# Gate and up of the second block's experts loaded whole: one 2 MB transfer each, each into its own slot, both slots freed together

## The reference

```python
def expert(x_e, w_gate, w_up, w_down):      # x_e: the tokens that chose this expert
    g = x_e @ w_gate                        # 1024 x 512, 2 MB
    u = x_e @ w_up                          # 1024 x 512, 2 MB
    return (silu(g) * u) @ w_down           # 512 x 1024, 2 MB
# out[token] += gate_weight * expert(...) for the two experts of each token
```

## Time and profile before

| | us |
|---|---|
| median of 3 runs | 2060.79 (2059.64 to 2061.04) |
| the profiled execution | 2061.98 |
| its span, first to last instruction | 2060.2 |
| TensorE busy | 1902.1 (92%) |
| second block's expert stage, first gate and up product to the last down product | 1557.8 to 2051 |

### The profile page before, as it was taken

One profiled execution on the slowest core, in us unless ns is written; L12 is line 12 of the kernel. 1 busy time (PEld: TensorE's weight loads), 2 busy tenths in 40 slices (PEclk: granted clock), 3 DMA queues, 4 the chain that ended last, 5 costly groups with the idle time before them and its releaser, 6 DMA issues.

```text
span 2060.2 us, 20805 instructions
## 1 busy us (share of the span) xinstructions
PE 1902.1 (92%) x8230; PEld 777.2 (38%) x8230; DVE 442.4 (21%) x1029; ACT 282.2 (14%) x534; POOL 22.4 (1%) x87
## 2 busy tenths in 40 slices
PE   7778999999999999999999888989988999999998
PEld 3443333333333333333333335647543333333333
DVE  1622111111111111111111123236522111111111
ACT  1311111111111111111111011130011111111111
POOL 3000000000000000000000000000000000000000
PEclk9888999999999999999999989999999999999999
DMA  9325999999999999999999473330244999999996
GB/s 304 154 97 213 412 408 415 410 407 416 412 407 413 410 410 408 416 411 408 415 410 407 209 274 134 128 118 1 82 166 174 400 414 404 409 404 419 403 410 249
DMA packets 82971, 667.63 MB, mean 324 GB/s; under 512 B 10384, under 2 KB 12192, under 8 KB 32640
## 3 DMA queue, kind: packets, MB, share of 16 engines
q1 hardware_dynamic: 78176, 664.84, 79.8%
q10 hardware_dynamic: 4416, 1.49, 0.3%
q0 software_dynamic: 352, 0.93, 0.2%
HBM read 666.19 MB, written 1.05 MB: 324 GB/s over the span
## 4 chain that ended last, share of the span: by engine, by line
PE 92%; ACT 4%; DVE 3%; issue 1%; DMA 0%; DVEq 0%; SPq 0%; ACTq 0%
PE ps L1299 54%; PE ps L1446 10%; PE ps L1359 6%; PE ps L1285 6%; PE ps L1180 3%; PE ps L1293 2%; PE ps L1249 1%; PE ps L1337 1%; PE ps L1330 1%; ACT Z L506 1%; ACT scr L510 1%; PE ps L1569 1%; PE ps L1164 1%; PE ps L1580 1%; PE ps L1603 1%
## 5 line engine op out<-in xcount | busy, mean ns | idle before, releaser
L1299 PE MATMUL ps<-ring,Z 128*64 128x512 f32 x4704 | 1051.2, 598 | 20.6 <-ACT Z L502 18.1
L1299 PEld LDWEIGHTS ps<-ring,Z 128*64 128x64 f32 x4704 | 342.3, 138 | 674.3 <-issue 648.2
L1359 PE MATMUL ps<-Z 64*128 64x512 f32 x520 | 129.2, 613 | 26.0 <-ACT Z L506 26.0
L1446 PE MATMUL ps<-ring,xT 128*128 128x512 f32 (+1 forms) x352 | 148.0, 581 | 1.5 <-DVE xT L653 0.8
L862 DVE TENSOR_SCALAR Z<-ps 128x512 f32<-128x512 f32 x33 | 22.8, 692 | 533.5 <-PE ps L1299 533.5
L1285 PE MATMUL ps<-xs,Z 128*64 128x512 f32 x536 | 131.1, 611 | 3.6 <-DVE Z L838 3.6
L1446 PEld LDWEIGHTS ps<-ring,xT 128*128 128x128 f32 x352 | 67.6, 193 | 79.2 <-issue 76.4
L506 ACT COPY Z<-ps 128x512 f32<-128x512 f32 x65 | 38.1, 586 | 333.4 <-PE ps L1299 333.4
L1359 PEld LDWEIGHTS ps<-Z 64*128 64x128 f32 x520 | 47.6, 186 | 87.4 <-issue 82.1
L849 DVE TENSOR_TENSOR Z<-ps,gcol 128x512 f32<-128x512 f32 x67 | 45.9, 686 | 148.0 <-PE ps L1293 148.0
L864 DVE TENSOR_SCALAR Z<-ps 128x512 f32<-128x512 f32 x33 | 22.8, 692 | 241.8 <-PE ps L1299 241.8
(11 more groups left out here) (343 smaller groups left out, 1106.8 us busy)
## 6 DMA issues: line engine op xcount, KB each, us to landing
ring<-in_w_gate SPq DMA_DIRECT2D x66, 2048.0 KB, 8.7
ring<-in_w_up SPq DMA_DIRECT2D x66, 2048.0 KB, 9.9
ring<-in_w_down SPq DMA_DIRECT2D x66, 2048.0 KB, 7.8
ring<-in_w_gate_experts SPq DMA_DIRECT2D x64, 1024.0 KB, 11.7
ring<-in_w_up_experts SPq DMA_DIRECT2D x64, 1024.0 KB, 13.9
ring<-in_w_down_experts SPq DMA_DIRECT2D x32, 2048.0 KB, 9.6
ring<-in_w_in SPq DMA_DIRECT2D x13, 2048.0 KB, 10.1
ring<-in_w_out SPq DMA_DIRECT2D x4, 2048.0 KB, 17.7
```

The costliest lines, as they stand in the source:

```text
L1299: last = pe.matmul(dst[CAP * j:CAP * (j + 1)], lhsT, rhs(j), start=start, stop=True, skip_group_check=True)
L1359: last = pe.matmul(bank(2 * a + j), back[CAP * j:CAP * (j + 1), a * P:(a + 1) * P], y[CAP * j:CAP * (j + 1), :], start=False, stop=True, s ...
L1446: last = pe.matmul(dst, lhs(c), rhs(c), start=c == 0, stop=c == nc_ - 1)
```

## The change

`expert_loads` for the second block now gives three transfers per expert: all of gate (2 MB, 16 KB per partition) into the first slot, all of up into the second, down as before. SyncE waits for the `free` of the second slot of an expert ahead of both, since only that is stepped any more. `gate_up` waits for both slots at its start, does the eight chunks (the same matmuls into the same bank, 32 records), and steps `free` of the second slot at the end. The loads of the first block, and all else, are untouched.

```diff
             loads = []
-            for q in range(2):
-                for i, name in enumerate((GATES[1], UPS[1])):
-                    v = src(name, "a (p c) n -> p (a c n)")
-                    loads.append((s0 + q, ring[:, s0 + q, 2048 * i:2048 * (i + 1)], v[:, 2048 * q:2048 * (q + 1)]))
+            for i, name in enumerate((GATES[1], UPS[1])):
+                loads.append((s0 + i, ring[:, s0 + i, :], src(name, "a (p c) n -> p (a c n)")))
...
-        LOADS = ((1,) * 6, (2, 2, 1))
+        LOADS = ((1,) * 6, (1,) * 3)
...
                         for s, dst, src in expert_loads(k, n * PAIR[k] + u, PER[k] * u):
-                            sp.wait_ge(free[s], n + FREE0[k][s])
+                            f = s + 1 if k == 1 and s % PER[k] == 0 else s
+                            sp.wait_ge(free[f], n + FREE0[k][f])
...
-                    for s in range(2):
-                        filled(s)
-                        v = ring[:, s0 + s, :].rearrange("p (g c n) -> p g c n", g=2, c=4)
-                        for c in range(4):
-                            chunk = 2 * c + s
-                            last = halves(bank(4).rearrange("p (g n) -> p g n", g=2),
-                                          picked[:, chunk * CAP:(chunk + 1) * CAP],
-                                          lambda j: v[:, :, c, 256 * j:256 * (j + 1)], s == 0 and c == 0)
-                        last.then_inc(freed(s), 1)
+                    filled(0)
+                    filled(1)
+                    v = ring[:, s0:s0 + 2, :].rearrange("p g (c n) -> p g c n", c=DC)
+                    for c in range(DC):
+                        chunk = 2 * (c % 4) + c // 4
+                        last = halves(bank(4).rearrange("p (g n) -> p g n", g=2),
+                                      picked[:, chunk * CAP:(chunk + 1) * CAP],
+                                      lambda j: v[:, :, c, 256 * j:256 * (j + 1)], c == 0)
+                    last.then_inc(freed(1), 1)
```

More of the change, by code:

```diff
@@ L297, in experts @@
                             if not seen[s]:
-                                sp.wait_ge(free[s], E // PAIR[k] + FREE0[k][s])
-                                sp.wait_ge(sem(f"over_free{k}_{s}"), i)
+                                f = s + 1 if k == 1 and s == 0 else s
+                                sp.wait_ge(free[f], E // PAIR[k] + FREE0[k][f])
+                                sp.wait_ge(sem(f"over_free{k}_{f}"), i)
                             seen[s] = 1
```

## The result

| | changed kernel | kernel before |
|---|---|---|
| first runs, median | 2075.75 us (4 runs, 2073.84 to 2081.13) | 2060.22 us (4 runs) |
| again, in a later session | 2078.83 us (5 runs, 2074.94 to 2080.71) | 2060.54 us (9 runs) |

The ratio is 1.0081 (95% interval 1.006 to 1.0101), and 1.0082 (1.0068 to 1.0095) again: slower by 0.8%. The forecast was slower by 0.4%, +8.4 us. The direction and the place are as forecast; the size forecast is about half of what came. The profiled execution took 2081.13 us, the longest of the nine, with a span of 2079.4.

A forecast was written before the change was run, and what follows sets the result against it. TensorE and DMA were both taken as near their limits, TensorE at 15.37 us per expert. A 0.3 us wait times 28 bursts gave +8.4 us, other terms 0: 2069.2 us on the median, range 2060.8 to 2076.

The forecast's parts named there:

- What decides: Second expert stage: slot B (second halves of gate and up) fills mean 1.05 us after product start; waiting there exposes it.
- The share of 0.45: DMA queue, second expert stage: landing time shortens by 0.45 of how much emptier a burst finds the queue; wait 0.3 us.
- The 0.1 us for longer rows: Second block's gate and up loads: 16 KB instead of 8 KB per partition saves 0.1 us of each burst.
- 12.25 us from start to down issue: Two-expert loop: 12.25 us from product start to its down product's end, when the next burst leaves.
- the loop of latency: Second expert stage: landing time stays however late a burst is issued; 0.53 us per expert, 14.7 us in all.
- The start of the stage: Expert 2's gate and up leave at 1567.43, land at 1580, wanted at 1586.85; cost 0, 7 us of cover.
- the merged freeing: Steady second expert stage: both slots are free 5 to 9 us before the down product's end SyncE awaits; cost 0.
- TensorE's own work: Gate-and-up product: same 32 records, one wait and one semaphore step less; 0, at most 0.05 us per expert.
- A: Rival, DMA queue: lateness paid once or not at all as the queue catches up; 2060.8 to 2062.8 us; chance 0.27.
- B: Rival: whole loop is latency, larger packets end less evenly; above 0.53 us per expert, 2076 to 2081 us; chance 0.06.
- C: Rival: faster by over 0.2%, needing idle time on TensorE to lose; chance 0.03.
- The Trainium skill's fixed cost per DMA: Second block's loads: some 2.0 us fixed per DMA; paid in series, two fewer transfers would take 4 us off each burst.

The follow-up runs named there:

- halves_both: Kernel before, its five transfers kept, gate-and-up product waiting for both slots at its start: 2079.16 us, ratio 1.0095; run again, 2078.78 us, ratio 1.0092.
- after_again: The changed kernel once more, unedited, against the kernel before: 2078.83 us, ratio 1.0082.
- pad_before: Kernel before plus one matmul of 360 columns of zeros, about 0.6 us, ahead of each second-block gate-and-up product: 2081.06 us, ratio 1.0099.
- pad_after: Changed kernel plus the same 0.6 us matmul per expert, placed ahead of its wait for ring: 2082.5 us, ratio 1.0104.
- pad_big: Kernel before plus 2.0 us of extra matmuls per expert, period 17.4 us: 2125.63 us (one run).
- order: Changed kernel with SyncE issuing the next but one expert's gate and up ahead of the earlier expert's down: 2060.39 us, ratio 1.0001 against kernel before.

## Why the prediction was right in direction and half in size

- **What decides.** Right: slot B was full on average 1.05 us after the product's start, and the wait for both slots at the start made this lateness a wait. halves_both shows it alone.
- **The share of 0.45** ("the time to landing is 19.52 - 0.1 less the share 0.45 of how much emptier the queue is found") is the step that failed. Before, the last landing of a burst lay 4.1 us on average behind the next burst's down issue, in the changed kernel's first profile 3.3: the queue was found 0.8 us emptier, and the bursts landed 0.1 us sooner (19.4 for 19.5), a share of 0.1. Half of the engines were done 0.6 us sooner, but the last of them lay 2.0 and not 1.4 us behind that, and took the gain away. In after_again it was 0.6 us emptier and they landed no sooner (19.6); pad_before gives 0.2. I had 0.27 from how bursts follow each other, called it diluted by noise and went up. The number read from the trace was nearer than the one it was "corrected" to. Nor is the share one number: pad_after gives 0.4 (19.0 us, the queue 1.2 emptier) and pad_big 0.5 (2.0 us sooner for 4.0 emptier), but the change moved the queue by less than 1 us. The DMA share of 1.00 and the 17.45 us of the one burst into an idle queue, which spoke for a plain queue, were misread: the first is an average over dips, the second the short one of the times that were found.
- **The 0.1 us for longer rows.** It did not show in the landings (19.4 and 19.6 us against 19.4 and 19.5 of the halves), and as time it is too small for these runs.
- **12.25 us from start to down issue.** Right, but the loop also has 0.14 us from the landing to TensorE's start, which the forecast left out: landing at 1681.96, start at 1682.10, the next burst at 1694.37, 12.4 in all.
- With these the forecast's own sum is (12.4 + 19.5) / 2 - 15.37 = 0.58 us per expert, 16 us over 28. Measured: 15.5 and 18.3 us over the two sets of runs. The forecast had 28 waits of 0.3 us; there were 17 in the first profile, 1.0 us on average. The end of the range that I had called the loop of latency (14.7) was nearest, and a little low. My sum of the likeliest lay between two ends, and one of them was close to what came.
- **The start of the stage, the merged freeing, TensorE's own work.** Each costed at 0, rightly: order has the merged freeing and the double wait and loses nothing.
- **Rivals.** A (paid once) did not come; B (above 0.53 per expert) came by its number, 0.55 and 0.65, and with its first reason, a longer period that does not shorten the landing. Its second, less even ends of larger packets, did not come: the 1 MB transfers lose as much. C did not come.
- **The Trainium skill's fixed cost per DMA** (DMA: Bandwidth & Descriptors, "Anatomy of one DMA") by an estimate from that page (2.0 us for each of two transfers less) would have the three transfers land 4 us before the five. The page gives the figure for DMAs issued by GpSimd; here SyncE issues them, and the trace shows no such gain: 19.4 and 19.6 us for three, 19.4 and 19.5 for five.

## What to carry to other kernels

A wait that moves ahead by half a product turns the lateness of the last landing at the new place into waiting, here 0.55 to 0.65 us per expert for landings 1.05 us late, since the loop covers two experts. So list the landings against the starts before merging two waits. The order of issue gave all of it back here at no cost: what is wanted first went first, and did not stand behind a wait for another slot. Where a product waits for a landing and its end triggers the next issue, sum the links of that loop with the time to landing as the trace has it, and do not shorten it for a queue that ought to be emptier unless a row shows by how much. A DMA share of 1.00 over a long window does not say that the engines are the bound: look at windows of a few us where one burst meets the next, and at how far apart the sixteen small records of its last transfer lie.

## What the runs showed that was not expected

The time to landing, told above: 17.5 us for 6 MB in one burst into a queue that has landed, mostly 18.6 to 20.5 when it is issued while the last burst still runs, with the same bytes. The difference lies mostly in the engines that finish last, up to 2.5 us behind all others in the burst shown.

The clock took a share in one execution. The changed kernel's longest profile (2081.13 us) has a window with a granted clock of 0.86, and in it a product of 8.77 us where all others take 7.09, right behind a wait of 1.91 us:

```profile
1971.03 8.77 PE L1299 MATMUL ps<-ring,Z 128*64 128x512 f32 x32 [1.91 <-DMA ring<-in_w_up_experts]
```
```profile
1968.00:1980.00 12.00, 10.09 (x40) 3.44 (x38) 0.60 (x2) 0.53 (x2) 0.00 (x0) 0.86 1.01 423
...
1971.03:1974.50 3.47, 3.47 (x10) 1.16 (x12) 0.00 (x0) 0.00 (x0) 0.00 (x0) 0.51 1.04 432
```

TensorE ran at the lower of its two levels (1.2 GHz) from the product's start to 1974.50, at a granted clock of 0.51, which cost 1.7 us once. Another wait of 1.94 us, at 1682.10, was followed by a product at 7.09 us, so such a wait does not always bring it; after_again kept the full clock from 1564 to 2029 us, with waits of up to 1.8.
